# Hybrid decoder step on one core: who issues the first token blocks, the parameter vectors and the second weight slab

## What is computed

```python
def short_conv(x, w_in, w_conv, w_out, buf):
    b_gate, c_gate, u = jnp.split(x @ w_in, 3, axis=-1)
    cu = c_gate * u
    ...                                  # three-tap convolution over tokens, times b_gate, @ w_out

def run_trunk(h, p, conv_bufs, past, norm_g, w_in, ...):
    for i in range(DEPTH):
        xn = rmsnorm(h, norm_g[i, 0])
        if i < N_A_LAYERS:
            y, buf = short_conv(xn, w_in[i], w_conv[i], w_out[i], conv_bufs[i])
...
```

## Time and profile before

| | |
|---|---|
| median of the runs | 3130.82 us (3130.07 to 3135.05) |
| the profiled execution's own time | 3130.13 us |
| its span, first to last instruction | 3128.5 us |
| TensorE busy | 3079.0 us, 98% |
| VectorE, ScalarE, GpSimd busy | 50%, 29%, 8% |
| mean granted TensorE clock | 0.996 of full speed |
| first TensorE instruction | 7.15 us |
| first matmul of the projection | 18.28 us |

### The profile page before, as it was taken

How to read it: one execution, slowest core, us unless ns; L and a number is a source line. 1 busy time by engine, 2 the same in 40 slices (tenths; PEclk the granted TensorE clock), 3 DMA queues, 4 the chain that set the end, 5 groups by cost and what they waited for, 6 DMA issues and landing times.

```text
span 3128.5 us, 51547 instructions
## 1 busy us (share of the span) xinstructions
PE 3079.0 (98%) x20352; PEld 2944.3 (94%) x20352; DVE 1566.7 (50%) x2613; ACT 903.4 (29%) x1600; POOL 262.2 (8%) x317
## 2 busy tenths in 40 slices
PE   8999999999999999999999999999999999999999
PEld 8999999999999999999978886569999999999998
DVE  5444284444444447453335665553744444444472
ACT  4111351111111116332235554343411111111262
POOL 1000010000000001000015551110100000000011
PEclk9999999999999999999999999999999999999999
DMA  3111111111111121113257865961111111111112
GB/s 107 45 44 47 42 41 41 48 41 47 48 41 48 41 62 41 41 48 112 98 153 157 163 120 227 395 243 39 43 42 47 48 41 48 41 48 47 57 48 71
DMA packets 229210, 247.46 MB, mean 79 GB/s; under 512 B 19061, under 2 KB 183925, under 8 KB 228994
## 3 DMA queue, kind: packets, MB, share of 16 engines
q1 hardware_dynamic: 204978, 164.65, 17.6%
q0 software_dynamic: 24016, 79.77, 8.3%
HBM read 209.50 MB, written 18.10 MB: 73 GB/s over the span
## 4 chain that ended last, share of the span: by engine, by line
PE 82%; DVE 4%; issue 2%; ACT 1%; DMA 1%; SPq 0%; DVEq 0%; POOL 0%; ACTq 0%
PE psum L2272 20%; PE psum L2274 20%; PE psum L2273 20%; PE psum L2856 2%; PE psum L2842 2%; PE psum L2298 2%; PE psum L2292 2%; PE psum L2293 2%; PE psum L2827 1%; PE psum L2828 1%; PE psum L2795 1%; PE psum L2797 1%; PE psum L2796 1%; PE psum L2975 1%; PE psum L2921 1%
## 5 line engine op out<-in xcount | busy, mean ns | idle before, releaser
L2272 PE MATMUL psum<-xs_hi,w_hi 128*128 128x384 f32 (+1 forms) x2592 | 848.8, 327 | 2.6 <-DVE w_lo L1477 2.4
L2274 PE MATMUL psum<-xs_hi,w_lo 128*128 128x384 f32 (+1 forms) x2592 | 845.5, 326 | 0.0
L2273 PE MATMUL psum<-xs_lo,w_hi 128*128 128x384 f32 (+1 forms) x2592 | 844.9, 326 | 0.0
L2272 PEld LDWEIGHTS psum<-xs_hi,w_hi 128*128 128x128 f32 x2592 | 486.7, 188 | 3.7 <-DVE w_lo L1477 3.7
L2273 PEld LDWEIGHTS psum<-xs_lo,w_hi 128*128 128x128 f32 x2592 | 486.7, 188 | 0.0
L2274 PEld LDWEIGHTS psum<-xs_hi,w_lo 128*128 128x128 f32 x2592 | 486.5, 188 | 0.0
L863 ACT ACTIVATE w_hi<-raw 128x1024 fp32r<-128x1024 f32 x192 | 202.4, 1054 | 618.6 <-DVEq L1500 596.9
L1858 DVE TENSOR_TENSOR y<-y,psum 128x384 f32<-128x384 f32 x528 | 268.8, 530 | 155.2 <-PE psum L2274 155.2
L2274 PE MATMUL psum<-hid_hi,w_lo 128*128 128x384 f32 (+1 forms) x1056 | 346.0, 328 | 0.0
L2272 PE MATMUL psum<-hid_hi,w_hi 128*128 128x384 f32 (+1 forms) x1056 | 345.6, 327 | 0.0
L2273 PE MATMUL psum<-hid_lo,w_hi 128*128 128x384 f32 (+1 forms) x1056 | 345.0, 327 | 0.0
(11 more groups left out here) (326 smaller groups left out, 4327.2 us busy)
## 6 DMA issues: line engine op xcount, KB each, us to landing
kpage<-in_cache_k SPq DMA_DIRECT2D x64, 512.0 KB, 8.5
v_page<-in_cache_v POOLq DMA_DIRECT2D x64, 512.0 KB, 6.1
raw<-in_w_gate SPq DMA_DIRECT2D x44, 512.0 KB, 3.7
raw<-in_w_up SPq DMA_DIRECT2D x44, 512.0 KB, 3.7
raw<-in_w_down SPq DMA_DIRECT2D x44, 512.0 KB, 3.8
raw<-in_w_in SPq DMA_DIRECT2D x24, 512.0 KB, 3.5
raw<-in_w_v SPq DMA_DIRECT2D x24, 512.0 KB, 3.3
raw<-in_w_ple_gate SPq DMA_DIRECT2D x16, 512.0 KB, 3.4
```

The costliest lines, as they stand in the source:

```text
L2272: M(out, wh, xh, start=first, stop=False)
L2273: M(out, wh, xl, start=False, stop=False)
L2274: return M(out, wl, xh, start=False, stop=last)
```

## The change

ScalarE now issues the first three token blocks and the four vector transfers, ahead of all its other work. GpSimd makes the identity first and issues what is left (blocks 3 to 7, the sample tokens, the two small weights). SyncE issues slab 0 as before and then waits until token block 2 has landed; slab 1 and, right behind it, slab 2 are issued after that. What is computed, and the order of all other instructions on each engine, is as before.

```diff
             for u, part in enumerate((0, 1, 2, 0, 1, 2)):
+                if u == 1:
+                    sp.wait_ge(x_landed[2], 16)
                 load(u, cols(w_in0, part * D + (u // 3) * P), C, P)
...
+            pool.memset(ident[:, :], 0.0).then_inc(consts, 1)
+            pool.memset(ones[:, :], 1.0).then_inc(consts, 1)
+            pool.memset(eps_c[:, :], EPS).then_inc(consts, 1)
+            pool.wait_ge(consts, 3)
+            mask(ident[:, :], [[-1, P]], 0, 1, ALU.not_equal, 1.0)
             for tb, (t0, n) in enumerate(TOKB):
+                if tb < 3:
+                    continue
                 dst = x_nat[:, tb, :] if tb < 8 else xs_nat[:, :]
                 src = x_prompt[0, t0:t0 + n, :] if tb < 8 else x_sample.rearrange("b t d -> (b t) d")
-                if tb == 3:
-                    for r0, n_, s in ((ROW_G, 8, norm_g.rearrange("l k d -> (l k) d")),
-                                      (ROW_KV, 1, g_kv.rearrange("(o d) -> o d", o=1)),
-                                      (ROW_CONV, 3, w_conv[0]),
-                                      (ROW_STATE, 16, state_conv[0].rearrange("b t d -> (b t) d"))):
-                        pool.dma_start(vec_nat[r0:r0 + n_, :], s).then_inc(vec_landed, 16)
                 pool.dma_start(dst, src).then_inc(x_landed[tb], 16)
-                if tb == 0:
-                    pool.memset(ident[:, :], 0.0).then_inc(consts, 1)
-                    pool.memset(ones[:, :], 1.0).then_inc(consts, 1)
-                    pool.memset(eps_c[:, :], EPS).then_inc(consts, 1)
-                    pool.wait_ge(consts, 3)
-                    mask(ident[:, :], [[-1, P]], 0, 1, ALU.not_equal, 1.0)
...
+            for tb in range(3):
+                act_e.dma_start(x_nat[:, tb, :], x_prompt[0, tb * P:tb * P + P, :]).then_inc(x_landed[tb], 16)
+                if tb == 0:
+                    for r0, n_, s in ((ROW_G, 8, norm_g.rearrange("l k d -> (l k) d")),
+                                      (ROW_KV, 1, g_kv.rearrange("(o d) -> o d", o=1)),
+                                      (ROW_CONV, 3, w_conv[0]),
+                                      (ROW_STATE, 16, state_conv[0].rearrange("b t d -> (b t) d"))):
+                        act_e.dma_start(vec_nat[r0:r0 + n_, :], s).then_inc(vec_landed, 16)
             act_e.wait_ge(consts, 3)
```

## The result

The changed kernel takes 3142.04 us (median of 7 runs, 3139.07 to 3145.96) beside 3131.51 us for the kernel before (7 runs on the same chip, 3128.29 to 3135.05): ratio 1.0034, with a 95% interval of 1.0024 to 1.0043. It is slower by 10.5 us; 3137.1 us was forecast, in a range of 3132.0 to 3139.6 us. The profiled execution took 3145.96 us, the slowest of the seven, for a span of 3144.3 us.

A forecast was written before the change was run, and what follows sets the result against it. TensorE, full from the first matmul on, was taken to bound the kernel, so a later start moves the end. Slab 1's rounding at 17.6 instead of 11.00 us adds 6.6 us to 3130.5: 3137.1 us, range 3132.0 to 3139.6.

The forecast's parts named there:

- What bounds the kernel: TensorE full behind the first matmul at 18.28 us, so any shift there moves the end equally.
- Step 1: ScalarE's issue of blocks 0 to 2 and vectors: block 0 lands near 5.0 us, 2 us earlier.
- Step 2: SyncE's slab 0 starves beside 4 KB packets, landing at 13.9 instead of 4.8 us; block 2 lands near 10 us.
- Step 3: SyncE's wait costs about nothing, as slab 1 stands behind slab 0 anyway; slab 1 lands at 17.6 us.
- Step 4: Slab 1's rounding starts at 17.6 instead of 11.00 us, so the first token tile starts 6.6 us later.
- check by volume: All transfers but slab 2 pass before slab 1 is through: 16.7 us, or 17.1 us with the lost 0.4 us.
- upper bound: Latest start of slab 1's rounding, 18.6 us, with 0.3 us for uneven engines: +7.6 us.
- rival A: Queues share by bytes, SyncE's small packets sent in bundles: slab 1 lands at 15.6 us, +4.7 us, 3135.2 us; 9%.
- B: Not slower: slab 1 has the engines to itself if block 2 lands before 7.6 us; -0.3 us, 3130.2 us; 6%.
- C: Slab 0 wins a head start, slab 1 lands at 14 us: +3 us, 3133.5 us; 11%.
- D: ScalarE's seven issues near 1.35 us each, slab 1 near 18.6 us: +7.6 us and up to 1 more, 3138.6 us; 8%.

The follow-up runs named there:

- e1: Changed kernel without SyncE's wait ahead of slab 1; ratio 1.0021 to the kernel before, first matmul 26.18 us.
- e2: Kernel before with only SyncE's wait for block 2 ahead of slab 1 added; ratio 1.0031, first matmul 28.11 us.
- e3: Changed kernel with GpSimd's w_f and b_f transfers issued later, behind the convolution rows' stores; ratio 1.0025 to the kernel before, first matmul 27.86 us.
- e5: Changed kernel with GpSimd's sample tokens, w_f and b_f held until slab 1 has landed; first matmul 26.33 us, one run.
- e6: Changed kernel with GpSimd's blocks from 3 on waiting until block 2 has landed; ratio 1.0008 to the kernel before, first matmul 21.24 us.
- e8: Changed kernel, vectors after blocks 0-2, slab 1 awaiting block 0, slab 2 samples, GpSimd's blocks block 1, slab 1 rounded behind first tile; ratio 0.9999 to kernel before.
- e4: Changed kernel with slab 1's two roundings moved later, ScalarE's behind block 5, VectorE's behind the first tile's low part; ratio 1.0007 to the kernel before.
- e7: Kernel before with a wait for block 2 ahead of slab 2 instead of slab 1; ratio 0.9994, first matmul 18.14 us.

## Why the prediction was wrong, step by step

**What bounds the kernel: right.** TensorE is full behind the first matmul, and the chain from slab 1's rounding to the token tile took 3.03 us against 3.02 forecast. In after and in the five experiments that keep the order of the roundings (e1, e2, e3, e5, e6) the first matmul comes 7.29 us behind the start of slab 1's rounding each time (before 7.28), and that shift is found again in every matmul up to 1561 us. Eight medians then stand within 1.6 us of the head's shift and e1's 2.4 us below it, where an interval is 3 us to a side.

**Step 1, block 0 by ScalarE: right.** Transposed at 4.88 us, forecast 5.0; seven issues took 2.9 us, forecast 2.4. The data began to flow at 2.1 us, not 2.9, and block 0 landed 2.4 us earlier than before though issued only 0.5 us earlier. But block 0 was not what the first matmul waited for.

**Step 2, "slab 0 now meets 4 KB packets from the start": failed.** Slab 0 landed at 6.8 us, not 13.9. The rule of one packet for one holds between a hardware queue and GpSimd's (192 to 193 in before, 115 to 117, 199 to 198, 185 to 187), and I carried it over to SyncE's queue against ScalarE's from the start, which no row showed. There, up to 3 us ScalarE's block moved alone (slab 0 had one packet by then, where I had given it 0.15 MB), from 3 to 4 us the two took turns, then slab 0 moved; and block 1, issued at 2.88 us, stood still until slab 0 was nearly through. Of the trace this is sure. What failed is not the taking of turns itself, but the assumption that both queues have packets to offer all the time from 2.9 us on. In e8, where block 1 was issued at 1.37 us with no vectors ahead of it, its first packet moved only at 5.1 us, and then SyncE's queue and ScalarE's did go one for one, from 6 to 6.5 us:

```profile
q10 hardware_dynamic: 44, 0.18, 87.5%
q1 hardware_dynamic: 44, 0.02, 14.8%
```

That the transfers of the two hardware queues are made ready for the engines one after the other is my reading of it, and no run shows it. The failure was worth little to slab 0's own users and much to block 2: at about 6 us both of ScalarE's last blocks were still to come, 1.05 MB, where I had 0.75 MB left at 5.5 us. They shared one for one with GpSimd, and the engines moved only 0.61 MB from 6 to 8 us. Block 2 landed at 13.3 us, not 10.

**Step 3, "the wait itself costs about nothing once (2) holds": failed with it.** (2) did not hold, so the wait did hold something: slab 0 was through at 6.8 us, and slab 1 stood for 6.5 us more behind a wait for block 2. But e1 shows that taking the wait away gives back only 1.2 us, since slab 1 is starved by GpSimd's blocks instead. So the sentence came out near right for after by luck, for another reason: whichever holds slab 1, the last of it comes only near the end of GpSimd's 2.9 MB. e2 shows that the wait can cost the whole by itself.

**Step 4, the sum: the size was off.** +9.1 us at the head for +6.6: slab 1 landed at 20.1 us, forecast 17.6. The check by volume (last byte at 17.1 us) took the engines to be full at 420 GB/s; after moved 0.61 MB from 6 to 8 us, 0.68 from 14 to 16 and 0.28 from 16 to 18, against 0.84 each, 0.95 MB in all or an estimated 2.3 us. That is about as much as the missing 2.5 us, though the runs confirm only a part of it one by one: about 1 us was the sample block (e5). The upper bound, +7.6 us, had allowed 0.3 us for uneven engines. The late issue has a price of its own too: from 14 to 16 us slab 1, issued at 13.29 us, moved 5 packets. Its first one came 2.6 us after the issue. Beside the same blocks that took 2.0, 1.7 and 1.4 us in e3, e4 and e5 and 3.5 us in e2; in e6, where no block of GpSimd was under way, it took 1.1 us. So this start-up is longer beside GpSimd's blocks, and not the same each time; by what means stays open.

Three slips in the working changed little. "1.37 MB by 13.2 us" is what moves between 9.4 and 13.2 us; the 0.77 MB left are right. The upper bound calls 17.6 us the last byte, which by the sum was 17.2 us. And rival A's 15.6 us is +4.6, not +4.7 us.

**The rivals.** B's condition (block 2 in before 7.6 us) was far off. A and C, gentler sharing between the hardware queues, were right that slab 0 escapes and wrong that this would help: slab 1 was as late as could be. D had the right side by another cause, ScalarE's issues, which were short. The Trainium skill ("DMA: Bandwidth & Descriptors", section on queues, rings and completion order) has each DMA engine take turns, packet by packet, between the rows for which it has work. From 4 to 5 us q10 had a block issued and moved 27 packets, 13 of them with data, beside 576 of q1's; so an issued transfer was not yet work for the engines, or the rule does not hold there. e8's 44 to 44 speak for the former: where both queues moved, they did take turns.

**The total** then came out 10.5 us, 1.4 us above the head; e2 and e3, with heads of 9.8 and 9.6 us, gave 10.6 and 8.4 us. I take this for the attention part's own spread; no experiment was made on it. Of the 4.9 us between 3142.04 us and the forecast, 2.5 are the head, 1.4 this, and 1.0 that the kernel before stood at 3131.5 us in these runs, where the forecast started from 3130.5 us.

## What to carry to other kernels

Before a transfer is moved to another queue or put behind a wait, ask which of the transfers the first full stage needs last, and what will stand on the DMA engines while it moves: here slab 1 had 3.4 us to spare, and both parts of the change spent more than that. Where packets of two sizes go one for one, as here, the load of small packets should be through before the large ones start, or these should be held back. And a late operand costs only as much as the order of instructions makes of it: moving one rounding behind work that doesn't need it gave back 5.75 of 9.1 us at the first matmul, and some 4.6 us once the wait behind it is counted.

## What the runs showed of the hardware

- ScalarE's and SyncE's queues did not take turns packet by packet throughout: from 4 to 5 us 576 packets of slab 0 moved beside 27 of ScalarE's, though a block of its was issued from 2.88 us on. In e8, with blocks 0 to 2 issued by 2.31 us, the next block's packets also came only behind 5 us; from then on the two queues went one for one.
- Data came sooner through a hardware queue than through GpSimd's: block 0's first packet moved 1.2 us after its issue by ScalarE (after), and 2.9 us after its issue by GpSimd (before).
- The same instructions took 1.8 times as long at the lower granted clock: the 24 transposes of blocks 3 to 5 took 5.08 us in e2 and 2.81 us in e7. One of them, from its start to its end, is 421 ns in the one and 273 ns in the other. In e2 TensorE stood idle for 10.76 us, and the granted clock was 0.50, the lower of the two levels (1.2 GHz), from 13.8 us until 27.4 us, when it rose again among the last of these transposes:

```profile
13.80:27.40 13.60, 4.65 (x22) 0.50 0.59 146
22.75:27.83 5.08, 5.08 (x24) 0.54 0.00 0
```

  In after the 24 took 5.18 us, and the clock's column says 1.00. That is no reading: the trace's first record of the clock begins at 26.90 us, and ahead of it the column shows 1.00 for want of one. The transposes of after are 421 ns long up to 26.5 us and 273 ns from 26.9 us on, so they fit the lower level too; in before the first record, and the change to 273 ns, come at 11.6 us. In after this cost nothing, since the first matmul waited for ScalarE's tile as well.
- GpSimd's issues of blocks are slower than ScalarE's: 5 blocks in 2.87 us, 0.57 us each, where ScalarE took 0.43 and 0.47 us.
